# First strip of a fused transformer block on Trainium2: another queue for the weights' first quarter, another order of loads, rounding and products

## The reference

```python
def rmsnorm(x, g):
    xf = x.astype(jnp.float32)
    y = xf * lax.rsqrt(jnp.mean(xf * xf, axis=-1, keepdims=True) + EPS)
    return (y * g.astype(jnp.float32)).astype(x.dtype)
...
        h = rmsnorm(x, ln1_g[l])
        proj = h @ w_in[l]
        qa, ka, va, qb, kb, vb, ga, gb = jnp.split(proj, offsets, axis=-1)
```

## Time and profile before

| what | value |
|---|---|
| three runs | 1323.9, 1321.1, 1321.42 us |
| median | 1321.42 us |
| profiled execution, span | 1321.2 us |
| PE busy | 1306.3 us (99%) |
| DVE busy | 925.2 us (70%) |
| ACT busy | 640.9 us (49%) |
| POOL busy | 70.0 us (5%) |
| read from HBM | 235.95 MB, 179 GB/s over the span |

### The profile page before, as it was taken

How to read it: one execution, slowest core, us unless ns; L and a number is a source line. 1 busy time by engine, 2 the same in 40 slices (tenths; PEclk the granted TensorE clock), 3 DMA queues, 4 the chain that set the end, 5 groups by cost and what they waited for, 6 DMA issues and landing times.

```text
span 1321.2 us, 17217 instructions
## 1 busy us (share of the span) xinstructions
PE 1306.3 (99%) x6973; PEld 1102.8 (83%) x6973; DVE 925.2 (70%) x1188; ACT 640.9 (49%) x839; POOL 70.0 (5%) x145
## 2 busy tenths in 40 slices
PE   8999999999999999999999999999999999999997
PEld 7887788888888888887888888888888877888886
DVE  6698777766656666788876666776666888676665
ACT  6777635443335444457554444444443566544441
POOL 4121000000000000000300000000000003000000
PEclk9999999999999999999999999999999999999999
DMA  8543565555555555653565555465555444655550
GB/s 303 192 159 87 138 238 166 190 193 190 194 208 199 191 191 191 191 145 100 171 223 191 192 191 190 154 236 193 187 193 186 160 128 127 231 190 192 188 188 33
DMA packets 155167, 238.11 MB, mean 180 GB/s; under 512 B 4248, under 2 KB 110768, under 8 KB 155088
## 3 DMA queue, kind: packets, MB, share of 16 engines
q1 hardware_dynamic: 154704, 236.47, 54.7%
q0 software_dynamic: 384, 0.54, 0.2%
HBM read 235.95 MB, written 1.05 MB: 179 GB/s over the span
## 4 chain that ended last, share of the span: by engine, by line
issue 86%; PE 10%; POOL 2%; POOLq 1%; ACT 1%; DMA 0%; DVE 0%; SPq 0%; DVEq 0%; ACTq 0%
PE ps L1561 2%; PE ps L1563 2%; PE ps L1562 2%; POOLq L552 1%; POOL drs L553 1%; PE ps L1705 1%; PE ps L1628 1%; POOL lrs L553 1%; PE ps L1714 0%; DMA raw<-in_w_in_dram 0%; PE ps L1729 0%; ACT ebuf L734 0%; PE ps L1683 0%; PE ps L1603 0%; PE ps L1604 0%
## 5 line engine op out<-in xcount | busy, mean ns | idle before, releaser
L527 DVE TENSOR_TENSOR wlo<-raw,whi 128x2048 fp32r<-128x2048 f32 x172 | 391.8, 2287 | 129.2 <-ACT whi L519 129.2
L519 ACT ACTIVATE whi<-raw 128x2048 fp32r<-128x2048 f32 x197 | 369.8, 1905 | 22.3 <-DMA raw<-in_w_up_dram 11.1
L1924 PE MATMUL ps<-xt_both,whi 128*128 128x512 f32 x1504 | 358.7, 390 | 0.0
L1924 PEld LDWEIGHTS ps<-xt_both,whi 128*128 128x128 f32 x1504 | 279.1, 188 | 55.9
L1929 PEld LDWEIGHTS ps<-xt_both,wlo 128*128 128x128 f32 x1504 | 193.4, 191 | 7.6
L1241 DVE TENSOR_REDUCE hid_a<-ps 128x512 f32<-128x1024 f32 (+1 forms) x98 | 115.3, 1177 | 119.5 <-PE ps L1929 119.3
L1929 PE MATMUL ps<-xt_both,wlo 128*128 128x256 f32 x1504 | 195.7, 283 | 0.0
L1561 PE MATMUL ps<-whi,ht_hi 128*128 128x512 f32 x480 | 187.7, 391 | 0.0
L1562 PE MATMUL ps<-wlo,ht_hi 128*128 128x512 f32 x480 | 187.3, 390 | 0.0
L1563 PE MATMUL ps<-whi,ht_lo 128*128 128x512 f32 x480 | 186.8, 389 | 0.0
L877 ACT ACTIVATE hid_b<-hid_a 128x512 f32<-128x512 f32 x40 | 25.2, 631 | 236.5 <-DVE hid_a L1241 236.5
(11 more groups left out here) (233 smaller groups left out, 1340.6 us busy)
## 6 DMA issues: line engine op xcount, KB each, us to landing
raw<-in_ffn_w_in_dram SPq DMA_DIRECT2D x80, 1024.0 KB
raw<-in_ffn_w_out_dram SPq DMA_DIRECT2D x44, 1024.0 KB
raw<-in_w_in_dram SPq DMA_DIRECT2D x36, 1024.0 KB
raw<-in_w_up_dram SPq DMA_DIRECT2D x16, 1024.0 KB
raw<-in_w_down_dram SPq DMA_DIRECT2D x16, 1024.0 KB
raw<-in_w_out_dram SPq DMA_DIRECT2D x8, 1024.0 KB
raw<-in_ffn_w_in_dram SPq DMA_DIRECT2D x16, 512.0 KB
raw<-in_w_out_dram SPq DMA_DIRECT2D x8, 512.0 KB
```

The source lines that it names most:

```text
L519: act.activation(whi[j][:, :], raw[j][:, :], ACT.Copy).then_inc(hi_done, 1)
L527: dve.tensor_tensor(wlo[j][:, :], raw[j][:, :], whi[j][:, :].bitcast(F32), ALU.subtract).then_inc(lo_done, 1)
L1924: pe.matmul(o(k).rearrange("p (j n) -> p j n", j=2), whi[w][:, block(b, k)], xt_both[:, :, b, :], start=b == 0, stop=False)
```

## The change

SP no longer loads the weights' first quarter; ACT issues that load as its first instruction. On SP x's second tile moves up, between the first strip's second and third quarters. ACT and DVE signal each block of the first strip by itself (`block_rounded`, `block_rest`; a unit's fourth block raises `hi_done` and `lo_done` as before) and take x's second tile between those blocks: its first half ahead of block 4, its second behind it. PE runs ten of the transposes of the identity in place of six, takes the first tile's blocks 0 to 3, turning x's second tile between them, then the second tile's products of blocks 0 to 3, and then blocks 4 to 7 with both tiles for each block. `used` is raised for the first unit after the second tile's block 3.

```diff
         def _(sp):
             sp.dma_start(xres[:, 0, :], x_r[:, 0, :]).then_inc(x_loaded[0], 16)
             sp.dma_start(g_rows[:, :], ln1_g[0, :].rearrange("(k p) -> k p", p=P)).then_inc(g_rows_loaded, 16)
-            for u in range(2):
-                sp.dma_start(rows_of(u)[:, 0:2, :], w_in_r[:, 4 * u:4 * u + 2, 0:BW]).then_inc(half_loaded[u], 16)
-                sp.dma_start(rows_of(u)[:, 2:4, :], w_in_r[:, 4 * u + 2:4 * u + 4, 0:BW]).then_inc(loaded[SLOT_OF[u]], 32)
+            sp.dma_start(rows_of(0)[:, 2:4, :], w_in_r[:, 2:4, 0:BW]).then_inc(loaded[SLOT_OF[0]], 32)
             sp.dma_start(xres[:, 1, :], x_r[:, 1, :]).then_inc(x_loaded[1], 16)
+            sp.dma_start(rows_of(1)[:, 0:2, :], w_in_r[:, 4:6, 0:BW]).then_inc(half_loaded[1], 16)
+            sp.dma_start(rows_of(1)[:, 2:4, :], w_in_r[:, 6:8, 0:BW]).then_inc(loaded[SLOT_OF[1]], 32)
...
+        def block_hi(act, k):
+
+            u, b = k // 4, k % 4
+            if b == 0:
+                act.wait_ge(half_loaded[u], 16)
+            elif b == 2:
+                act.wait_ge(loaded[SLOT_OF[u]], 32)
+            scaled_hi(act, u, (b,)).then_inc(block_rounded if b < 3 else hi_done, 1)
...
+        def block_lo(dve, k):
+            u, b = k // 4, k % 4
+            wait_block(dve, block_rounded, hi_done, k)
+            scaled_lo(dve, u, (b,)).then_inc(block_rest if b < 3 else lo_done, 1)
...
         def _(act):
+            act.dma_start(rows_of(0)[:, 0:2, :], w_in_r[:, 0:2, 0:BW]).then_inc(half_loaded[0], 16)
             xt_act(act, 0, toks=(0,), halves=(0,))
             act.wait_ge(g_ready, 1)
-            half_split_hi(act, 0, 0)
+            for k in (0, 1):
+                block_hi(act, k)
             xt_act(act, 0, toks=(0,), halves=(1,))
-            half_split_hi(act, 0, 1)
-            for h in range(2):
-                half_split_hi(act, 1, h)
+            for k in (2, 3):
+                block_hi(act, k)
+            xt_act(act, 0, toks=(1,), halves=(0,))
+            block_hi(act, 4)
+            xt_act(act, 0, toks=(1,), halves=(1,))
+            for k in (5, 6, 7):
+                block_hi(act, k)
             rms_act(act, 0, (0,))
-            xt_act(act, 0, toks=(1,))
...
+            for k in (0, 1):
+                first_products(pe, "hi hi", (k,), 0)
+                first_products(pe, "lo hi", (k,), 0)
+            first_products(pe, "hi lo", (0, 1), 0)
+            for k in (2, 3):
+                first_products(pe, "hi hi", (k,), 0)
+                first_products(pe, "lo hi", (k,), 0)
+                xt_half_pe(pe, 0, 1, k - 2, xres)
+            first_products(pe, "hi lo", (2, 3), 0)
+            for what in ("hi hi", "hi lo", "lo hi"):
+                m = first_products(pe, what, range(4), 1)
+            m.then_inc(used, 1)
+            for k in range(4, KD):
+                for what in ("hi hi", "lo hi"):
+                    for t in range(TT):
+                        first_products(pe, what, (k,), t)
+                for t in range(TT):
+                    m = first_products(pe, "hi lo", (k,), t)
+            m.then_inc(used, 1)
...
-            for _ in range(6):
+            for _ in range(10):
                 pe.transpose(ps[:, 3, 0:P], ident[:, :], ident[:, :])
```

More of the change, by code:

```diff
@@ L296, in build @@
         half_loaded = [sem(f"half_loaded{j}") for j in range(2)]
-        half_hi = sem("half_hi")
-        half_lo = sem("half_lo")
+        block_rounded = sem("block_rounded")
+        block_rest = sem("block_rest")
         g_rows_loaded = sem("g_rows_loaded")
@@ L502, in scaled_lo, with wait_block @@
             return m
[L504 to L511, removed]
+        def block_hi(act, k):
[5 more added lines that the diff above has]
+            scaled_hi(act, u, (b,)).then_inc(block_rounded if b < 3 else hi_done, 1)
+        def wait_block(eng, blocks, units, k):
+            u, b = k // 4, k % 4
+            if b < 3:
+                eng.wait_ge(blocks, 3 * u + b + 1)
+            else:
+                eng.wait_ge(units, u + 1)
+        def block_lo(dve, k):
+            u, b = k // 4, k % 4
+            wait_block(dve, block_rounded, hi_done, k)
+            scaled_lo(dve, u, (b,)).then_inc(block_rest if b < 3 else lo_done, 1)
         def split_hi(act, u):
@@ L1391, in _ @@
             xt_dve(dve, 0, toks=(0,), halves=(0,))
-            half_split_lo(dve, 0, 0)
+            for k in (0, 1):
+                block_lo(dve, k)
             xt_dve(dve, 0, toks=(0,), halves=(1,))
[L1394 to L1397, removed]
+            for k in (2, 3):
+                block_lo(dve, k)
+            xt_dve(dve, 0, toks=(1,), halves=(0,))
+            block_lo(dve, 4)
+            xt_dve(dve, 0, toks=(1,), halves=(1,))
+            for k in (5, 6, 7):
+                block_lo(dve, k)
             for s in range(S1_SOLID):
@@ L1613, in first_tile, with first_products @@
             return m
[L1615 to L1625, removed]
+        def first_products(pe, what, ks, t):
+            o, tok = ps[:, t, :], slice(t * P, (t + 1) * P)
+            for k in ks:
+                if k % 4 == 0 and what == "hi hi":
+                    pe.wait_ge(xt_hi_done, 2 * t + k // 4 + 1)
+                if k % 4 == 0 and what == "lo hi":
+                    pe.wait_ge(xt_lo_done, 2 * t + k // 4 + 1)
+                if t == 0 and what == "hi hi":
+                    wait_block(pe, block_rounded, hi_done, k)
+                if t == 0 and what == "hi lo":
+                    wait_block(pe, block_rest, lo_done, k)
@@ L1626, in pairs_of_first_tile @@
                 x = xt_lo if what == "lo hi" else xt_hi
                 w = wlo if what == "hi lo" else whi
-                pe.matmul(o, x[:, k, tok], block_of(w, u, k % 4), start=what == "hi hi" and k == 0,
-                          stop=what == "hi lo" and k == KD - 1)
+                m = pe.matmul(o, x[:, k, tok], block_of(w, k // 4, k % 4), start=what == "hi hi" and k == 0,
+                              stop=what == "hi lo" and k == KD - 1)
+            return m
         def first_projection(pe):
-            pairs_of_first_tile(pe, 0, "hi hi")
@@ L1634, in first_projection @@
[L1634 to L1645, removed]
@@ L1646, in first_projection @@
-            pairs_of_first_tile(pe, 3, "hi lo")
-            first_tile(pe, 0, 0, 1, 1)
+            for k in (0, 1):
+                first_products(pe, "hi hi", (k,), 0)
+                first_products(pe, "lo hi", (k,), 0)
+            first_products(pe, "hi lo", (0, 1), 0)
+            for k in (2, 3):
+                first_products(pe, "hi hi", (k,), 0)
+                first_products(pe, "lo hi", (k,), 0)
+                xt_half_pe(pe, 0, 1, k - 2, xres)
+            first_products(pe, "hi lo", (2, 3), 0)
```

## The result

| | before | changed |
|---|---|---|
| median, five runs each | 1321.42 us | 1326.16 us |
| lowest to highest | 1321.1 to 1323.9 us | 1325.36 to 1326.66 us |
| ratio, 95% interval | | 1.0030 [1.0019, 1.0041] |
| span of the profiled execution | 1321.2 us | 1323.6 us |
| its own time | not recorded | 1325.39 us |

The changed kernel is slower by 0.3%, some 4 us, clear of the 0.2% that a measurement tells. 1320.8 us was forecast, in a range up to 1322.3. The table ahead of the prediction took the span for the time of that execution, which was wrong by these 1.8 us.

What follows compares the result with a forecast made beforehand. PE was taken as the bound, busy 1306.3 of 1321.2 us. Terms +0.6 (blocks) + 1.7 (clock) - 0.9 (waits) - 0.8 (constants) = 0.6 us won, from median 1321.42 to 1320.8 us; range 1319.6 to 1322.3.

Steps and rivals of the forecast that it cites:

- - 0.8: Sum's term for the constants: issued later, they delay DVE's angles and the third strip's wlo, costing 0.8 us.
- First product at 8.4.: PE's start: with blocks signalled singly, the first product comes at 8.4 instead of 8.99, 0.6 us won.
- rival B: PE's start: x's first tile late at 6.5, clock stays low; 0.4 to 1.9 us slower, 1321.8 to 1323.3; chance 0.2.
- They cost nothing unless the clock is low.: Ten identity transposes before the first product: four more take 0.44 us of idle time; 2.2 us for ten at low clock.
- ACT's last block at 14.9.: First strip's rounding on ACT: the last block ends at 14.9, not 13.1 as before.
- I take 25.0: Last constant's landing ahead of DVE's angles: 25.0, between 24.5 and 26.0, with half a microsecond for traffic.
- upper bound of 5.4: Last constant's travel: at most the first constant's 5.4 us from issue to landing, so landed by 26.0.
- The second strip at 21.35, 1.4 us won.: PE's second strip: starts at 21.35 instead of 22.75, after waiting 0.7 us for its wlo.
- 22.75 + 48 x 0.227 = 33.6: Third strip's start in the earlier trace: second strip's start plus 48 product steps, the point where gains are counted.
- +1.7 (clock).: First products on PE: gap shrinks from 2.0 to about 0.4, clock stays up, 1.7 us won.
- ACT is no bound there: Third strip's start: ACT, waiting for POOL's norm at 27.9, has read strip one at 30.4, before PE at 33.
- case A: Third strip: constants land at 26.0, wlo done at 33.9, 0.35 us slower, 1321.8; chance 0.25 together with no change.

Runs made afterwards that it cites:

- const_early: Changed kernel, POOL issuing the constants' DMAs after the first unit's last block instead of the second's; 1322.32 us, 1.0003 to the kernel before.
- no_extra: Changed kernel without the ten transposes of the identity behind x's first tile; 1326.05 us, 1.0030 to the kernel before.
- weights_held: Changed kernel, SP loading the third strip's second unit only after the constants have landed; 1322.76 us, 1.0004 to the kernel before.
- b_const_late: Kernel before, POOL waiting for the rounding of x's second tile before issuing the constants; 1330.46 us, 1.0062 to the kernel before.
- b_again: The kernel before, unedited, measured and profiled once more; 1321.79 us, 0.9997, profiled span 1319.7 us.
- b_const_early: Kernel before with the constants' DMAs one unit earlier, after the first unit's last block; 1321.98 us, 0.9999 to the kernel before.
- angles_later: Changed kernel, DVE computing angles, masks and lambda sums behind the third strip's splits instead of ahead; 1323.92 us, 1.0013 to the kernel before.
- g_between: const_early with g turned between the halves of x's first tile and four identity transposes instead of ten; 1321.31 us, 0.9996 to the kernel before.
- both: g_between with DVE's angles, masks and lambda sums between the splits of the third strip's two units; 1321.4 us, 0.9995 to the kernel before.
- quarter_on_sp: const_early with the weights' first quarter back on SP, ahead of the second; 1322.06 us, 0.9999 to the kernel before.
- g_first: const_early with g's rows loaded ahead of x's first tile on SP, four identity transposes instead of ten; 1321.76 us, 0.9996 to the kernel before.

## Why the prediction was wrong

The mechanism was the right one and the sizes were not. The prediction named the last rounded block, the constants behind it, DVE's angles and the third strip as the way on which the gain would be eaten; every link of it is in the trace of the change. But it called the result 0.6 us won, where 2.3 us were lost against that trace and 4.7 against the median. The step that failed is the price of the constants, "- 0.8" in its sum; const_early measured it at 2.7 us by the traces (third strip at 33.4 instead of 36.1) and 3.8 by the medians. Step by step:

- **"First product at 8.4."** It came at 9.75. x's tile was there at 4.8 (forecast 5.1) and the quarter at 6.0, sooner than the 7.5 that I took. I had not costed g's eight rows. Their landing rose from under 4.7 to 5.8, and PE turns g ahead of x, so PE stood idle from 4.4 to 5.8. This was rival B with the wrong culprit: B wanted x at 6.5.
- **"They cost nothing unless the clock is low."** It was low: ten transposes took 2.34 us and ended after ACT's first block. no_extra prices them in its trace at 0.7 us for the constants' issue and 1.1 us at the third strip; the rest came back, since without them the products bear the low level. What failed is the assumption that PE is at the full level when it turns x: the clock rose at 10.8 us.
- **"ACT's last block at 14.9."** 16.3, by the same 1.4 us. With it POOL's first DMA at 16.64 instead of 15.2.
- **"I take 25.0"** for the last constant. 28.0: 1.4 of the 3.0 us by the late issue, 1.5 by the travel of 5.9 us instead of the 4.4 taken, beyond even the upper bound of 5.4. I had seen that the weights' load would be released at 15 (it was 16.9, and 21.9 before) and would stream beside the constants, and priced it at half a microsecond. weights_held shows some 2 us of travel for it, and b_const_late up to 8.5 us. The bound from the row of the first constant was no bound: that DMA had 1 KB and met another traffic.
- **"The second strip at 21.35, 1.4 us won."** 22.66, 0.1 won; of no weight, since the third strip's start was set elsewhere. The base of that start, 22.75 + 48 x 0.227 = 33.6, is 0.2 low: in the trace it is 33.8.
- **"+1.7 (clock)."** The low stretch in the earlier trace rows isn't in the typical execution; in b_again, b_const_late and b_const_early the clock was full there. The gain existed only against the trace, not against the median, so the time had to come out some 1.5 us above a sum made on that trace, and I took the median as if it belonged to it. A profile whose own time isn't known should be given that margin.
- **No term for what a wait costs behind itself.** b_const_late and no_extra lost 2.4 and 1.6 us in the strip behind the wait, to a fall of the clock. The changed kernel's own profile has no such fall, its other executions may have.
- **"ACT is no bound there"**, with POOL's norm at 27.9. The norm began at 28.54, behind the constants' landing, and ACT had read the first strip only at 32.95. In the change DVE's split was later still; in angles_later it was the next thing to wait for.
- **What was right:** the place of the loss, the order of its links, DVE's 2.8 us idle ahead of the angles as the sign of case A, a last block after 16 as that of B. What happened is nearest to B, with g's rows in the place of x's tile: B had the last constant issued at 22.2 (22.03), landed at 27.6 at the latest (28.0) and the third strip's wlo done by 35.5 (35.9). Its upper end, 1323.3, is still 2.9 us under the median: 0.4 of that is the later third strip (2.3 us against 1.9), 1.5 the trace taken for the median, and 0.8 lies between the changed kernel's profile and its median.

Worked by measured terms, at DVE's first angle instruction against b_again: POOL's issue 3.9 us later (16.64 against 12.72), travel 1.7 us longer (5.9 against 4.2), less the 1.4 us by which the last constant was early in b_again (landed at 22.3, angles at 23.7): 4.2, measured 4.3 (28.06 against 23.73). At the third strip's start 3.9 of it are left.

With this cost taken away (const_early, g_between, both, weights_held) the changed order is as fast as the old one and no faster. Starting the products sooner (7.86 in g_between, 7.22 in both, against 8.31 in b_again) and interleaving the second tile buys nothing beyond noise in the medians. The second strip's start is set by its own unit: ACT begins to round it at 15.6 to 17.3 us in each of these kernels but one, DVE splits it for 2.7 us behind that, and PE waits 0.3 us for the end of it in every trace of the changed order. Only in the trace of both was it sooner (14.5), and there half a microsecond was kept.

The medians hide one thing. The kernel before took 1323 us or more in 24 of the 86 executions beside these runs (one of 7465 us left out), at a mean clock of 0.996 to 0.998, and b_const_early in 5 of 11. The highest of the 55 executions of const_early, quarter_on_sp, g_first, g_between and both is 1322.91. So the changed start seems to win what the prediction wanted of the clock, about 2 us, in those executions that have the fall of the earlier trace rows. No trace here shows one of them besides the first, so that it is this fall isn't shown.

## What to carry to other kernels

When a signal is made earlier or later, list everything else that is released by it: here a counter raised for the matmuls also let POOL's ten small loads go, and a buffer freed five microseconds sooner (16.9 against 21.9) put a megabyte of weights in their way. Keep small constants off the order of an engine that splits weights, or have slack for the longest travel seen and not for the mean. And before a gain is read from one profiled execution, know that execution's own time: a stretch at the low clock that occurs in one run of several is no target, or counts only by its share of the runs. A wait may cost more than itself, if the clock falls in it or behind it.

## What the runs showed of the hardware

- The time to landing of the same 256 KB broadcast load, issued last of ten, was 3.9 to 8.6 us: 3.9 (before, weights_held) and 4.2 (b_again) where the weights' queue was empty or thinning, 5.5 to 5.9 in the change, no_extra and angles_later, 6.5 to 8.6 where weights streamed throughout (const_early 6.5, b_const_early 7.0, g_first and quarter_on_sp 7.5, g_between 8.1, both 8.6), 8.5 where their stream came back in the midst of it (b_const_late).
- POOL's work behind a drain started only after its own loads had landed: the norm at 30.17, 0.6 us after the last landing, in b_const_late, and at 28.54, again 0.6 after, in the change. It is 0.5 to 0.7 in all eleven traces in which the norm didn't wait for ACT's sums. That the drain is what waits wasn't tried apart. I had counted on POOL being free once the loads were issued.
- With a second issuing queue the rate in the first microseconds was higher (319 to 344 against 274 to 312 GB/s from 2 to 6), and it delayed by about a microsecond whatever the first queue had issued second.
- PE's clock fell at the wait before the third strip in two traces: behind 1.9 us of idle time in no_extra (1.6 us lost) and within 5.4 us of it in b_const_late (2.4 us lost). Behind 2.25 us in the change it stayed full.
- PE's clock rose at different moments of kernels with the same start: the ten transposes took 2.34 us in the change (rise at 10.8) and 1.82 in weights_held (rise at 8.8), where the first product found the full level. Nothing but transposes had run there before it:

```profile
7.66 1.82 PE L2034 MATMUL ps<-ident 128*128 128x128 f32 x10
9.23 1.17 PE L1656 MATMUL ps<-whi,xt_both 128*128 128x512 f32 x4
```

The Trainium skill ("TensorE: Matmul & The Clock Gate", on transposes) says that transpose mode doesn't count as PE being busy. By that rule the level couldn't have risen before 9.23; four products at a step of 0.26 say that it had, so the trace disagrees here, as the prediction's rows did.

What stays open: why the constants' loads keep the DMA engines busy at so low a rate even when alone. It wasn't tried apart.
